# Scan's decay rows through DRAM, and the linear attention's norm in pieces

## The reference

```python
def step(S, inp):                       # one chunk of 128 tokens
    xc, ac, bc, cc = inp
    acum = jnp.cumsum(ac, axis=-1)
    seg = acum[..., :, None] - acum[..., None, :]
    Lm = jnp.exp(jnp.where(causal, seg, -jnp.inf))
    cb = jnp.einsum('bign,bjgn->bgij', cc, bc)
    y = jnp.einsum('bgij,bghij,bjghp->bighp', cb, Lm, xc)
    y = y + jnp.einsum('bign,bghpn,bghi->bighp', cc, S, jnp.exp(acum))
    last = acum[..., -1:]
    S = (S * jnp.exp(last)[..., None]
         + jnp.einsum('bjgn,bghj,bjghp->bghpn', bc, jnp.exp(last - acum), xc))
    return S, y
```

## Time and profile before

| | us |
|---|---|
| median of 3 runs | 3270.27 |
| lowest, highest | 3269.34, 3273.44 |
| the profiled execution, its time | 3276.36 |
| its span in the trace | 3274.6 |

### The profile page before, as it was taken

How to read it: one execution, slowest core, us unless ns; L and a number is a source line. 1 busy time by engine, 2 the same in 40 slices (tenths; PEclk the granted TensorE clock), 3 DMA queues, 4 the chain that set the end, 5 groups by cost and what they waited for, 6 DMA issues and landing times. The chain is left out here.

```text
span 3274.6 us, 40804 instructions
## 1 busy us (share of the span) xinstructions
PE 3120.2 (95%) x16356; PEld 2558.1 (78%) x16356; DVE 1330.9 (41%) x1993; ACT 942.4 (29%) x1671; POOL 1249.2 (38%) x400
## 2 busy tenths in 40 slices
PE   5999989999998999999989999999999998999998
PEld 4878977788987778887756888888888775788886
DVE  6566443836634122233366422232222336632223
ACT  3355442435543211102445211011110245521101
POOL 1322334323233454444330444445444434144442
PEclk9999998999999999999989999999999998999999
DMA  5311313422131222222110222232223221022222
GB/s 228 123 66 52 94 53 149 154 71 80 45 102 39 77 93 100 90 89 102 66 51 13 79 94 98 88 104 81 99 87 97 84 78 39 14 90 90 98 89 70
DMA packets 43466, 279.70 MB, mean 85 GB/s; under 512 B 5240, under 2 KB 5624, under 8 KB 16248
## 3 DMA queue, kind: packets, MB, share of 16 engines
q1 hardware_dynamic: 42688, 270.84, 23.6%
q10 hardware_dynamic: 632, 6.82, 0.7%
HBM read 275.54 MB, written 2.10 MB: 85 GB/s over the span
## 5 line engine op out<-in xcount | busy, mean ns | idle before, releaser
L1886 PE MATMUL PS<-x_parts,w_parts 128*128 128x512 f32 x4224 | 962.0, 390 | 4.0 <-ACT x_parts L726 3.9
L1827 POOL TENSOR_TENSOR w_parts<-w_raw,w_parts 128x2048 fp32r<-128x2048 f32 (+1 forms) x152 | 644.5, 4240 | 811.8 <-DVE w_parts L1961 757.5
L1886 PEld LDWEIGHTS PS<-x_parts,w_parts 128*128 128x128 f32 x4224 | 794.1, 188 | 173.4 <-issue 4.7
L136 POOL TENSOR_TENSOR w_parts<-w_raw,w_parts 128x2048 fp32r<-128x2048 f32 (+1 forms) x98 | 449.9, 4591 | 1003.1 <-ACT w_parts L127 969.0
L328 PE MATMUL PS<-x_parts,w_parts 128*128 128x512 f32 x2784 | 697.7, 397 | 13.6 <-POOL w_parts L136 4.6
L328 PEld LDWEIGHTS PS<-x_parts,w_parts 128*128 128x128 f32 x2784 | 522.2, 190 | 133.2 <-issue 18.7
L1927 PE MATMUL PS<-hidden_parts,w_parts 128*128 128x512 f32 x2112 | 482.9, 390 | 0.0
L1927 PEld LDWEIGHTS PS<-hidden_parts,w_parts 128*128 128x128 f32 x2112 | 396.2, 188 | 83.8 <-issue 1.9
L1968 DVE TENSOR_TENSOR ffn_buffers<-PS,ffn_buffers 128x512 f32<-128x512 f32 x88 | 60.9, 692 | 733.0 <-PE PS L1886 708.9
L331 PE MATMUL PS<-w_parts,x_parts 128*128 128x256 f32 x2304 | 296.1, 288 | 2.2 <-POOL w_parts L136 2.2
L331 PEld LDWEIGHTS PS<-w_parts,x_parts 128*128 128x128 f32 x2304 | 282.1, 192 | 15.4 <-issue 9.8
(11 more groups left out here) (394 smaller groups left out, 3178.0 us busy)
## 6 DMA issues: line engine op xcount, KB each, us to landing
w_raw<-in_w_gu SPq DMA_DIRECT2D x88, 1024.0 KB, 4.7
w_raw<-in_w_in SPq DMA_DIRECT2D x70, 1024.0 KB, 4.8
w_raw<-in_w_d SPq DMA_DIRECT2D x64, 704.0 KB, 4.0
w_raw<-in_w_out SPq DMA_DIRECT2D x24, 1024.0 KB, 4.8
m_all<-in_w_next SPq DMA_DIRECT2D x14, 1024.0 KB, 8.0
m_all<-in_w_gate SPq DMA_DIRECT2D x8, 1024.0 KB, 4.9
m_all<-in_w_next ACTq DMA_DIRECT2D x2, 1024.0 KB, 11.1
x_all<-in_x ACTq DMA_DIRECT2D x1, 2048.0 KB, 13.1
```

Of the source, the lines that this page charges most:

```text
L136: pool.tensor_tensor(parts[:, self.slot(u), 1, 0:n], raw[:, self.slot(u), 0:n], parts[:, self.slot(u), 0, 0:n].bitcast(F32), ALU.subtract) ...
L1827: pool.tensor_tensor(WP[:, b, 1, 0:n], RAW[:, b, 0:n], WP[:, b, 0, 0:n].bitcast(F32), ALU.subtract).then_inc(self.low, 1)
L1886: return pe.matmul(PS[:, 2 * b + g, :], WP[:, slot(b), w, c:c + P], XS[:, x, k, :], start=start, stop=stop)
```

## The change

The selectors, their load and `spread_decay` are gone. ACT, from its own queue, stores `afm` to a DRAM tensor `decay_rows` (one row of 16 x 128 per chunk) and loads for each step the 1024 values of its group, the same row into all 128 partitions, into one of two slots of `rows`. The relu reads `rows` and not PSUM. In the mixer ACT copies the linear attention's output times the gain out of PSUM right after squaring it; reciprocal and both products are done on DVE in eight pieces of 128 columns in `after(s)` for s below 8. `turn_compressed` moves by one place: 0 into the middle of job jr, 1 and 2 into jr + 1, and 3 behind both jobs and the first two scores. Four tiles are rounded for the output in another order and grouping.

```diff
             @block.sync
             def _(sp):
-                sp.dma_start(sel[0:SH, :], dr["sel"]).then_inc(s_sel, 16)
@@ tensor engine, scan
-                def spread_decay(s):
-                    c, g = steps[s]
-                    if s == 0:
-                        pe.wait_ge(s_sel, 16)
-                        pe.wait_ge(s_xtc, 8)
-                        pe.wait_ge(s_smt, 3)
-                    else:
-                        pe.wait_ge(s_sg, s)
-                    for h in range(HG):
-                        hh = g * HG + h
-                        last = pe.matmul(PS[:, 4 + h // 4, (h % 4) * P:(h % 4 + 1) * P],
-                                         sel[0:SH, hh * P:(hh + 1) * P], afm[:, c * P:(c + 1) * P],
-                                         start=True, stop=True)
-                    last.then_inc(s_bc, 1)
-                spread_decay(0)
                 for s in range(8):
                     proj.run(pe, jv + 2 + 2 * s, tokens)
-                    if s + 1 < 8:
-                        spread_decay(s + 1)
                     proj.run(pe, jv + 3 + 2 * s, tokens)
                     outputs(s)
@@ scalar engine, scan
+                act.dma_start(decay_rows.rearrange("c (h j) -> h c j", h=SH),
+                              split3(afm, NT)).then_inc(s_dw, 16)
+                def load_decays(s):
+                    c, g = steps[s]
+                    source = decay_rows[c:c + 1, g * D:(g + 1) * D].broadcast_to([P, D])
+                    act.dma_start(rows[:, s % 2, :], source).then_inc(s_dr[s % 2], 16)
                 for j in range(jx, jv + 2):
+                    if j == jx + 2:
+                        act.wait_ge(s_dw, 16)
+                        for s in range(2):
+                            load_decays(s)
                     evacuate(j)
@@ decays(s)
-                    act.wait_ge(s_bc, s + 1)
+                    act.wait_ge(s_dr[s % 2], 16 * (s // 2 + 1))
                     for h in range(HG):
                         last = act.activation(seg[:, s % 2, h * P:(h + 1) * P],
-                                              PS[:, 4 + h // 4, (h % 4) * P:(h % 4 + 1) * P], ACT.Relu,
+                                              rows[:, s % 2, h * P:(h + 1) * P], ACT.Relu,
                                               bias=acum[:, c, g * HG + h:g * HG + h + 1], scale=-1.0)
                     act.wait_ge(s_sg, s + 1)
+                    if s + 2 < 8:
+                        load_decays(s + 2)
@@ mix_tokens
-            order = (6, 7, 4, 5, 0, 1, 2, 3)
+            order = (4, 5, 6, 7, 0, 1, 2, 3)
@@ tensor engine, mixer
-                proj.run(pe, jr, tokens, {0: each(turn_compressed, 0), 4: each(turn_compressed, 1)})
-                proj.run(pe, jr + 1, tokens, {0: each(turn_compressed, 2), 4: each(turn_compressed, 3)})
+                proj.run(pe, jr, tokens, {4: each(turn_compressed, 0)})
+                proj.run(pe, jr + 1, tokens, {0: each(turn_compressed, 1), 4: each(turn_compressed, 2)})
                 pe.wait_ge(evacuated, jo)
                 pe.wait_ge(s_iv, 4)
                 for s in range(2):
                     att.score(pe, s)
+                turn_compressed(3)
@@ scalar engine, mixer
                             act.activation(chunks(sg[t], odd), gla_output(t, odd), ACT.Square).then_inc(s_s2, 1)
+                        for odd in range(2):
+                            act.activation(chunks(og[t], odd), gla_output(t, odd), ACT.Copy,
+                                           scale=p2("gla_g")[:, t:t + 1]).then_inc(s_iv, 1)
@@ take_output
-                        if n == 0:
-                            act.wait_ge(s_fin, 2)
-                        else:
-                            act.wait_ge(s_pw, 2)
-                        for k in order[2 * n:2 * n + 2]:
+                        if n:
+                            act.wait_ge(s_fin, 8)
+                        act.wait_ge(s_pw, n + 1)
+                        for k in order[1:4] if n else order[0:1]:
                             act.copy(XS[:, 0, k, :], M[:, k, :]).then_inc(parts.high, 1)
@@ vector engine, mixer
-                for t in range(2):
-                    dve.wait_ge(s_r, t + 1)
-                    link(dve.reciprocal(sg[t], sg[t]))
-                    for odd in range(2):
-                        dve.scalar_tensor_tensor(chunks(og[t], odd), gla_output(t, odd), p2("gla_g")[:, t:t + 1],
-                                                 chunks(sg[t], odd), ALU.mult, ALU.mult).then_inc(s_iv, 1)
@@ after(s)
-                    if s < 2:
-                        dve.wait_ge(s_iv, 4)
-                        dve.tensor_tensor(M[:, 6 + s, :], M[:, 6 + s, :], og[s], ALU.mult).then_inc(s_fin, 1)
+                    if s < 8:
+                        t, c = divmod(s, NT)
+                        at = slice(c * P, (c + 1) * P)
+                        if c == 0:
+                            dve.wait_ge(s_r, t + 1)
+                            dve.wait_ge(s_iv, 2 * t + 2)
+                        link(dve.reciprocal(sg[t][:, at], sg[t][:, at]))
+                        link(dve.tensor_tensor(og[t][:, at], og[t][:, at], sg[t][:, at], ALU.mult))
+                        dve.tensor_tensor(M[:, 6 + t, at], M[:, 6 + t, at], og[t][:, at], ALU.mult).then_inc(s_fin, 1)
```

17 lines of the change are left out of this document (8 added, 9 removed).

## The result

The changed kernel takes **3239.56 us** (median; 3239.22 to 3244.90), the kernel before in the same comparison 3271.86: 32.3 us less, a ratio of 0.9903 with a 95% interval of 0.9886 to 0.9920. The prediction was 3237. In the profiled executions the span fell from 3274.6 to 3238.0, by 36.6.

The account below looks back on a forecast made before the run. PE, busy 95% of the span, was taken as the bound. Scan 20 us plus mixer 12.8 us gave 33 us off the profiled 3276.4, and 3237 for the median; 3216 to 3256 was given 8 in 10.

Parts of the forecast that it names:

- Start of the scan: Up to the first output products: ACT's relus, exp and the first weighting set the time; gain 3.4 us per layer.
- Step 0 to 1: First-chunk scan step, between starts of output products: DVE's chain is short, the 1.97 us spread is saved; 8.6 us long.
- last rival: Two shifts meet badly: PE's new idle places lower its clock, or rounding hits every weighting; most of 33 us lost; chance 0.05.
- Steps 2 to 3 and 4 to 5: Later-chunk scan steps beside POOL's lowering, hanging on DVE and POOL: a loss of 0.4 us and no gain.
- first rival: PE is the only bound: DVE and POOL slip past each other, every spread is paid out; 3224 us, chance 0.18.
- Step 3 to 4: Later-chunk scan step: DVE's chain ends at O + 10.15 (O: output products' start), outputs wait; gain 1.15 us.
- Step 5 to 6: Scan step scaling one operand less (last chunk): DVE done at about O + 9.0 (O: output products' start); keeps 1.97 us.
- Row loads: Eight 512 KB loads per layer on ACT's queue, issued two steps ahead: cost 0 up to roughly 9 us each.
- Mixer, gain: Second block, compressed softmax's end to first turned probabilities: 9.25 us, a gain of 11.0 and 12.3 us by layer.
- Mixer, pieces: Eight norm pieces of 1.6 us on DVE lengthen the attention's first groups: 4.8 and 5.7 us lost by layer.
- pieces at 2.3 us each: Rival: the norm's pieces on DVE cost what the stall gave, 11 us back; 3248 us, chance 0.20.
- Slow row loads: Rival: loads reading one 4 KB row 128 times become the bound; at 15 us each 3304 us, chance 0.05.

Follow-up runs that it names:

- filler: Changed kernel plus PE products nobody reads: one ahead of each layer's first output products in the scan, two at the fourth and sixth; 3236.89 us.
- taking POOL away: Changed kernel with POOL's lowering of weight units in the scan cut to 64 of 2048 columns; 3222.04 us.
- turn_order_alone: Changed scan, and of the mixer part only the last turn moved behind the first scores; norm whole on DVE ahead of them, as before; 3264.27 us.
- scan_alone: Kernel before with only the scan part of the change, the second block's norm as before; 3265.25 us.
- mixer_alone: Kernel before with only the mixer part of the change, the scan as before; 3259.28 us.
- POOL later: POOL's twelve low-part subtractions start after DVE takes the first block's last attention output; on the changed kernel 3244.05 us, with three reorderings too 3212.98 us.

## Why the prediction was right

The predicted time was 2.6 us off, but errors offset one another: between the two profiled executions the scan gave 16.3 us where 20 was said, the mixer 16.2 where 12.8 was said, and 4 more came outside both; these two lie 36.6 us apart, the medians 32.3, since the profiled execution of before lay above its median, as the prediction took into account. That the sum came so near was luck: its two parts were 3.7 us too high and 3.4 too low, the 4 us outside were in no term, and the same scan took 69.4 to 76.4 us per layer in other executions, where the changed kernel's profiled one had 71.0 and 71.7.

- **Start of the scan**: 3.4 said; 5.1 in the first layer and 3.6 in the second (from the last turn of x to the first outputs, 13.1 and 11.6 us before, 8.0 after). The first layer gave more since there the kernel before ran its first job behind PE's idle time at the lower clock, 4.63 us.
- **Step 0 to 1**: 8.57 said, 10.05 and 10.12 measured. This is the step that failed. I had noted that PE gets a new idle time of over 1 us, and gave it no price but in the last rival (a lower clock, chance 0.05). The granted clock of this step is 0.83; filler brings 8.51 at 1.00, and so does a start without the idle time. Six other first layers show that the price is not always asked.
- **Step 1 to 2**: 8.57 said, 8.4 measured.
- **Steps 2 to 3 and 4 to 5**: 11.8 and 11.4 said; 11.4 and 12.3, 11.49 and 11.83 measured. POOL met DVE in both, as said, and taking POOL away shortens both to 9.3. The prediction also held that which of the two starts first moves the block along DVE's chain and the step by 0.7 us: in the second layer L1499 was blocked (5.17), in the first L1499 took 0.69 and L1509 was (4.28), and the steps differ by 0.9. What I called the first rival (PE the only bound) came true for the later steps once DVE's weighting was put elsewhere: 9.25 each, and 3223.55 in all.
- **Step 3 to 4**: 10.25 said, 10.19 and 11.29. In the second layer PE stood idle for 2.89 us ahead of it and the granted clock was 0.85, in the first 2.00 us and 1.00; with filler 10.19 and 10.20.
- **Step 5 to 6**: 9.43 said, 11.04 and 9.36. In the first layer PE had stood idle for 1.98 us ahead of the sixth output products, for a weighting that had met POOL in the step before, and then ran at the lower clock (L1185 1.91 us, two jobs 6.79). Free of POOL, as said, but not of the clock (0.85) behind a wait that POOL had made; filler brings 9.36. In the second layer the wait was 2.30 us and the clock stayed at 1.00.
- **Row loads**: 4.4 us, no wait; up to about 9 us was said to cost nothing, and a load of 512 KB from one row of 4 KB took 1.1 us more than one from separate rows. **Relus**: eight take 2.46 us from SBUF, before 2.17 from PSUM: 0.29 more, where I took 0.1. The Trainium skill's figure, page "VectorE: DVE Perf Modes", section "The TRN2 errata", which gave an estimate of 0.35, was the better one.
- **Mixer, gain**: 11.0 and 12.3 said to the first turned probabilities, 9.2 and 10.6 measured. The order of work was as forecast; the eight weighings ran at the lower clock (5.54 us at a granted clock of 0.69, where turn_order_alone has 3.85 in the same layer at 1.00), behind another idle time of PE, 2.06 us ahead of the last turn. No run put filler there.
- **Mixer, pieces**: groups of 12.4 and 12.5 said, 11.01 and 11.03 measured, 11.24 and 11.03 in the second layer. The mechanism was right (DVE busy 10.76 of 11.03), the term mis-sized: I added 0.5 us of waits to a DVE that then has none, and took the old operations at the 5.5 us for which they keep DVE busy where they stand apart. Back to back each starts before the one ahead of it ends, and four steps of old work take 11.03 - 4 x 1.51 = 4.99. The third group lost nothing (10.43 against 10.56). That gives 1.5 us of loss in the first layer and 2.6 in the second, where I had 4.8 and 5.7.
- **Rivals**: pieces at 2.3 us each are refuted by the 1.51. Slow row loads are refuted. "The two shifts meet badly" was right in kind, with new idle places and a lower clock, and wrong in size: filler gave back 5.4 us in the scan, not most of the 33.
- **Outside**: the 4 us that came behind the first block's attention are of the kind shown above. DVE's product there (L1548 before) took 1.66 us in both layers of before's profiled execution and 0.82 and 0.84 in that of the changed kernel: 1.7 of the 4. They come with the changed scan (scan_alone 4.4, mixer_alone 0.0), but other kernels with that scan have from -11 to 6 us there, so it is no fixed saving; how the scan brings them, and the rest of the 4 us, is open.

## What to carry to other kernels

When work is taken off the engine that bounds a loop, look at what the next engine does last in its chain, and whether it could do that first: the change took up to 33.6 us off PE in the two scans; 16.3 were paid out, and 31 once DVE's weighting stood ahead of its wait. Give every new idle place on PE a second price, for a slower clock behind it, and let it be a range: here nothing, 1.6 or 3.2 us for the same 1.66. And where two waits cover one another, either edit alone looks worthless: here 1.7 and -3.0 us, together 16.2.

## What the runs showed of the hardware

A DVE product with both operands in SBUF that arrives in the middle of a row of POOL subtractions (1.3 us each, no gap between them) usually gets in between two of them. In 24 such places, two in each of twelve kernels, it took about 0.8 us nine times and about 1.65 us fourteen times (0.69 with POOL later), and once 12.66 us, when all that was left of the row of twelve went first. The Trainium skill, page "SBUF — State Buffer", section "Who interferes with whom", says that the one that issues first keeps the ports for its whole instruction. The traces agree for single instructions (L1499 took 5.17 us beside a lowering of 4.63); the 12.66 us are longer than any instruction of POOL (5.7 us at most), and no run here shows what decides when the other engine has its next one ready.

The scan of the changed kernel is not the same from execution to execution: 69.4 to 76.4 us per layer for the same instructions. Two things differ: which of DVE's operations meets a lowering (step 2 to 3 at 11.40 or 12.29), and how far the clock falls behind PE's idle places (step 0 to 1 at 8.50, 10.1 or 11.7). In the three profiled executions with the weighting moved ahead it took 62.27 to 63.91 in all six layers, and the steps of the later chunks never differed by more than 0.01 us.
